# Moving the tail stores and the pooled sums inside the cache loop of a hybrid decoder step

## The chip, the cores and the metric

The kernel runs on one core of one Trainium2 chip. The metric is the device time of one launch in microseconds, as the median of several runs. The core has five engines that work side by side and meet only through semaphores: TensorE (PE, with its weight loads PEld), VectorE (DVE), ScalarE (ACT), GpSimd (POOL) and SyncE (SP). DMAs are issued here from SP, ACT and POOL.

## The reference

The reference is one step of a two-layer decoder trunk on 256 prompt tokens and 8 x 8 sample tokens, all in float32. Each layer computes

```
h   = RMSNorm(x) @ W_in                    # q, k, v | z, xBC, dt | xp
mix = [ StickBreakingAttn(q,k,v) | Mamba2-SSD(z,xBC,dt) | MultiScalePool(xp) ]
x   = x + mix @ W_out
x   = x + W_down( silu(dwconv3(RMSNorm(x) W_gate)) * RMSNorm(x) W_up )
```

The attention of the samples reads 2048 cached tokens a sequence in pages of 128 tokens. `xBC` goes through a causal convolution of width 4, whose last three input rows a sequence are returned (`new_ssm_conv_*`, here the convolution's tails). The pool takes, for four groups of channels, the mean over windows of 2, 4, 8 and 16 tokens minus the token itself, and returns the last 15 input rows a sequence (`new_pool_*`, the pooling's tails). Other results are the keys, the values and the states.

## The kernel before

A layer has four stages with a meeting of all engines between them: the input projection, the mixer (the cache loop), the output projection, and the feed-forward part. The change lies in the mixer alone, which runs once a layer, so twice.

**The cache loop.** Sample attention goes through 128 pages of keys and 128 of values, eight of each a chunk, 16 chunks. The loop is written out by hand as slots: slot s is chunk `qn = s // 8`, position `k = s % 8`. In a slot TensorE transposes one key page (`key_page`, L1122) and multiplies one value page of the chunk two back (`value_page`, L1163), and then does the one step of the rest of the mixer that the table `MIX` (L88) gives for that slot (`step`). ACT, DVE and POOL run through the same slots in the same order, each with its share of the step. The steps' results go alternately into two PSUM banks; TensorE's next step in a bank waits until the one before it was read (`mix_read`).

Steps that matter here: `c` (decays of one quarter of the heads), `y` (SSD output), `s` (the state after the first 128 tokens; ACT copies it into `sT`, L826), `n` (the final prompt state), `pool` (the pool's matmul, L1271), `ctail` (three steps: transpose the convolution's tails, DVE copies them into `ctail`, L1769) and `ptail` (two steps: the pooling's tails of prompt and samples into `ptailP` and `ptail`, L1772). `ctail` and `ptailP` lie in the bytes of `sT`. So ACT may write `sT` at step `("s", 0)`, slot 19, only when all four tail stores have landed (`tail_stored`, L825).

**POOL's queue.** POOL does everything in program order: the loads of value pages (`value_in`, L503; eight buffers; V(q,k) below is page k of chunk q; V(0,k) are loaded ahead of the loop, and V(1,k) is issued at slot 16+k, when TensorE has used V(0,k), and read at slot 24+k), the pooled sums of four groups (`pooled(g)`, L506 to L528: one, two, three and four adds and five instructions behind them, with a drain of the engine after each add), the weighted x of a block (`weighted_x`, L537), the stores of the tails, the gating of y by z (`gate`, L562 to L566, with drains as well) and later the sample states. Before, `pooled` stands at slots 1, 6, 9 and 11, the convolution's stores and the load of `poolw` at slot 13, and the pooling's stores at slot 17.

Of the kernel before, what the change touches and what calls it, by code (L numbers as in the profile page):

```python
# [16 lines left out]
F32 = mybir.dt.float32  # L17
# [29 lines left out]
CVD = SSW + 2 * NG * NS  # L47
# [23 lines left out]
for _t in PARTS:  # L71
# [13 lines left out]
MEETS = 4  # L85


MIX = {0: ("b", 0), 1: ("x", 0, 0), 2: ("x", 0, 1), 3: ("cum", 0), 4: ("dec",), 5: ("ctail", 0),  # L88
# [3 lines left out]
       23: ("b", 1), 24: ("x", 1, 0), 25: ("x", 1, 1), 26: ("cum", 1), 27: ("pool", 0), 28: ("pool", 1), 29: ("pool", 2),  # L92
# [6 lines left out]
for _i in range(2, NB):  # L99
    _s = 67 + 5 * (_i - 2)  # L100
    MIX.update({_s: ("T", _i, 0), _s + 1: ("Y", _i - 1), _s + 2: ("T", _i, 1), _s + 3: ("N", _i - 1, 0),
                _s + 4: ("N", _i - 1, 1)})
# [16 lines left out]
def build(nc, a, o):  # L119

    with ExitStack() as ctx:
        at = [16512]

        def sb_at(name, shape, dt, offset):
            return nc.alloc_sbuf_tensor_at(name, shape, dt, offset=offset)
# [12 lines left out]
        def sem(name):  # L138
            return ctx.enter_context(nc.semaphore(name))


        x = sb("x", [P, KT, TOK])
# [4 lines left out]
        ah_at = at[0]  # L147
# [5 lines left out]
        w_at = at[0]  # L153
# [67 lines left out]
        y = sb_at("y", [P, SST, TOK], F32, hh_at + 4 * TOK * 4)  # L221
# [16 lines left out]
        dec = sb_at("dec", [P, SST, 10], F32, raw_at + 32256)  # L238
        bm = sb_at("bm", [SAMP, 2, NG * NS], F32, ah_at)
        sel = sb_at("sel", [SSH, SST, P], F32, ah_at + 31744)  # L240
        ctail = sb_at("ctail", [27, CVD], F32, w_at + 24576)

        p1 = sb_at("p1", [P, XPL], F32, ah_at + 25600)
        p2 = sb_at("p2", [P, XPL], F32, ah_at + 27520)
# [4 lines left out]
        ptailP = sb_at("ptailP", [PH, POOLW], F32, w_at + 30720)  # L249
        ptail = sb_at("ptail", [P, POOLW], F32, ext_at + 1920)  # L250
# [59 lines left out]
            sem("y_sq"), sem("y_sq_s"), sem("y_ms"), sem("y_root"), sem("y_normed"), sem("y_high"))  # L310
        s_loaded, s_stored = [sem(f"s_loaded{i}") for i in range(4)], [sem(f"s_stored{i}") for i in range(4)]
        s_decayed, s_bm, snew_stored = sem("s_decayed"), sem("s_bm"), sem("snew_stored")
        tail_stored, ftail_T, ftail_out = sem("tail_stored"), sem("ftail_T"), sem("ftail_out")

        passed = sem("passed")
# [3 lines left out]
        def alone(eng):  # L319

            eng.sem_inc(passed, 1)
# [124 lines left out]
        def _(pool):  # L446
# [23 lines left out]
            with pool.Fori(0, DEPTH) as l:  # L470
# [37 lines left out]
                def pooled(g):  # L508

                    win = WINS[g]  # L510
                    src, w, bufs = xp[:, g, :], 1, [p1, p2]
                    while w < win:
                        dst = bufs[0][:]
                        bufs.reverse()
                        pool.tensor_tensor(dst[:, 2 * w - 1:], src[:, 2 * w - 1:], src[:, w - 1:XPL - w], ALU.add)
                        pool.drain()  # L516
                        src, w = dst, 2 * w
                    news = pdiff[:, g, SEQ:TOK].rearrange("p (b t) -> p b t", b=NB)
                    pool.tensor_scalar(pdiff[:, g, 0:SEQ], src[:, PH:PH + SEQ], 1.0 / win, None, ALU.mult)
                    pool.tensor_scalar(news, src[:, SEQ + PH:].rearrange("p (b t) -> p b t", b=NB)[:, :, PH:], 1.0 / win,  # L520
                                       None, ALU.mult)
                    pool.drain()

                    pool.tensor_tensor(pdiff[:, g, 0:16], src[:, PH:PH + 16], con[:, K_CNT + 16 * g:K_CNT + 16 * g + 16],
                                       ALU.mult)
                    pool.drain()
                    pool.tensor_tensor(pdiff[:, g, 0:SEQ], pdiff[:, g, 0:SEQ], xp[:, g, PH:PH + SEQ], ALU.subtract)
                    pool.tensor_tensor(news, news, xps[:, g, :, PH:], ALU.subtract).then_inc(p_diff, 1)  # L528
# [21 lines left out]
                def pool_tails_out():  # L550
                    read(pool, l, "ptail", 0)
                    read(pool, l, "ptail", 1)
                    pool.dma_start(o["new_pool_prompt"][l, 0], ptailP[:]).then_inc(tail_stored, 16)
                    pool.dma_start(o["new_pool_sample"][l].rearrange("b k c -> (b k) c"), ptail[0:NB * PH, :]
                                   ).then_inc(tail_stored, 16)

                def gate(blk):

# [37 lines left out]
                for qn in range(CHUNKS + 3):  # L596
                    for k in range(8):
                        slot = 8 * qn + k
                        if 2 <= qn <= CHUNKS:
                            value_in(qn - 1, k)  # L600
                        if slot in (1, 6, 9, 11):
                            pooled((1, 6, 9, 11).index(slot))
                        for blk in range(3):
                            if slot == SLOT["cum", blk] + 2:
                                weighted_x(blk)
                        if slot == SLOT["ctail", 2] + 1:
                            conv_tails_out()
                        if slot == SLOT["ptail", 1] + 1:
                            pool_tails_out()
                        for blk in range(2):  # L610
                            if slot == SLOT["y", blk, 3] + 1:
                                gate(blk)
                        if slot == SLOT["n", 1] + 1:
                            read(pool, l, "n", 0)
                            read(pool, l, "n", 1)
                            pool.dma_start(o["new_ssm_prompt"][l, 0].rearrange("(j e) p n -> (e p) j n", e=2), snew[:]
                                           ).then_inc(snew_stored, 16)
                        for i in range(NB):
                            if slot == SLOT["N", i, 1] + 1:
                                state_out(i)  # L620
                            if slot == SLOT["T", i, 1] + 1:
                                state_rows(i)
                                state_decay(i)
# [8 lines left out]
                for half in range(2):  # L632
# [5 lines left out]
                pool.dma_start(o["new_ffn_conv_prompt"][l, 0], ftail[0:2, :]).then_inc(tail_stored, 16)  # L638
                pool.dma_start(o["new_ffn_conv_sample"][l].rearrange("b k c -> (b k) c"), ftail[2:18, :]
                               ).then_inc(tail_stored, 16)  # L640
                pool.wait_ge(tail_stored, l * 96 + 96)
                alone(pool)
                meet(pool, "pool", stage(l, M_FFN))
            pool.wait_ge(last_out, 12)
# [7 lines left out]
        def _(act):  # L652
# [51 lines left out]
            with act.Fori(0, DEPTH) as l:  # L704
# [109 lines left out]
                def step(s):  # L814

                    if s not in MIX:
                        return
                    kind, *at = MIX[s]
                    b, bank = USE[MIX[s]][0], ps[MIX_BANKS[USE[MIX[s]][0]]]
                    if kind == "s":  # L820
                        h = at[0]
                        written(act, l, *MIX[s])
                        if h == 0:
                            act.wait_ge(tail_stored, l * 96 + 64)
                            alone(act)  # L825
                        act.activation(s1T[:, h * 512:(h + 1) * 512] if h < 2 else  # L826
                                       sT[:, 1, (h - 2) * 512:(h - 1) * 512], bank[:], ACT.Copy).then_inc(mix_read[b], 1)
                    elif kind == "pool":
                        written(act, l, *MIX[s])
                        act.activation(hh[:, SBT + SST + at[0], :], bank[:, 0:TOK], ACT.Copy,  # L830
                                       scale=par[:, C_PS + at[0]:C_PS + at[0] + 1]).then_inc(p_hi, 1)
                    elif kind == "T":
                        i, h = at
                        written(act, l, *MIX[s])
                        if i >= 2 and h == 0:
                            written(act, l, "Y", i - 2)
                        act.activation(sT[:, i % 2, h * 512:(h + 1) * 512], bank[:], ACT.Copy).then_inc(mix_read[b], 1)

                def exponentials(blk, j):

                    b, bank = USE["c", blk, j][0], ps[MIX_BANKS[USE["c", blk, j][0]]]
                    T, n = tokens(blk)[1], 4 * blk + j
                    act.wait_ge(c_min, l * 12 + n + 1)
                    for i in range(4):
                        mm = act.activation(seg[n % 4][0:T, i, 0:T], seg[n % 4][0:T, i, 0:T], ACT.Exp,
                                            bias=tk[0:T, 2, 4 * j + i:4 * j + i + 1])
                    mm.then_inc(c_exp, 1)
                    if blk:
                        dst = cs[j][:] if blk == 1 else csS[:, 4 * j:4 * j + 4, :]
                        act.activation(dst, bank[:, 0:4 * T].rearrange("p (h t) -> p h t", h=4), ACT.Exp  # L850
                                       ).then_inc(mix_read[b], 1)
# [1165 lines left out]
```

## Time and profile before

| | us |
|---|---|
| median of 3 runs | 3483.42 (3478.25 to 3485.31) |
| profiled execution, its own time | 3491.93 |
| its span in the trace | 3490.4 |
| PE busy | 3264.5 |
| DVE busy | 1921.2 |
| ACT busy | 1338.9 |
| POOL busy | 379.5 |

The profiled execution's own time is its span and 1.5 us around it; it lies 8.5 us above the median of the runs. Times in the trace are counted from the start of the span. The mixer stage of the first layer goes from about 340 to 648 us, that of the second from about 2056 to 2360 us. A row of a timeline has the start, the duration, the engine, the line, the operation with its operands, the count, and in brackets how long the engine was idle before and what it waited for.

### The profile page before, as it was taken

How to read it: one execution, taken by the hardware profiler on the slowest of the kernel's cores; microseconds unless marked ns; L12 is line 12 of the kernel's file. 1: busy time of each engine (PE TensorE's matmuls, PEld its weight loads, DVE VectorE, ACT ScalarE, POOL GpSimd, SP SyncE). 2: the span in 40 equal slices, each digit the busy share in tenths (PEclk: the TensorE clock that was granted, in tenths of full speed). 3: DMA queues.
4: the chain of work that ended last, by engine and by line, in shares of the span. 5: the costliest groups of instructions: out<-in, count | busy, mean ns of one | idle time of the engine just before them, and what ended most of it. 6: DMA issues, size and time to landing. Idle time of an engine off the chain costs nothing.

```text
span 3490.4 us, 66373 instructions
## 1 busy us (share of the span) xinstructions
PE 3264.5 (94%) x23775; PEld 3055.9 (88%) x23775; DVE 1921.2 (55%) x3351; ACT 1338.9 (38%) x1641; POOL 379.5 (11%) x465
## 2 busy tenths in 40 slices
PE   5999899899999999999889988979899999999995
PEld 5999566689999999999879975649899999999994
DVE  5574555346654665466356645454666446645654
ACT  2453555433432333233235535553344333333331
POOL 2000544110000000000020025530200000000000
PEclk8999898899999999999989999999899999999997
DMA  5442698634444444444434437985344444444441
GB/s 154 137 129 91 209 292 284 217 122 133 148 146 155 145 151 150 145 155 132 126 117 133 133 116 220 323 280 169 108 150 145 155 145 151 149 146 155 144 135 44
DMA packets 467566, 553.41 MB, mean 159 GB/s; under 512 B 20044, under 2 KB 413869, under 8 KB 466625
## 3 DMA queue, kind: packets, MB, share of 16 engines
q1 hardware_dynamic: 436354, 461.42, 41.5%
q0 software_dynamic: 26112, 88.93, 8.1%
q8 instruction: 105, 1.72, 0.2%
q10 hardware_dynamic: 4898, 0.55, 0.1%
q14 instruction: 97, 0.79, 0.1%
HBM read 534.46 MB, written 16.38 MB: 158 GB/s over the span
## 4 chain that ended last, share of the span: by engine, by line
PE 86%; issue 4%; DVE 3%; ACT 2%; DMA 1%; POOLq 1%; POOL 1%; DVEq 1%; ACTq 0%
PE ps L937 25%; PE ps L938 25%; PE ps L939 25%; PE ps L1122 2%; PE ps L1163 2%; PE ps L1132 1%; PE ps L1295 1%; PE ps L1283 1%; PE ps L1277 1%; DVE hl L1416 0%; POOLq L516 0%; POOLq L502 0%; DMA xrow<-in_x_sample 0%; PE ps L975 0%; ACT wz L804 0%
## 5 line engine op out<-in xcount | busy, mean ns | idle before, releaser
L1374 DVE TENSOR_TENSOR wl<-raw,wh 128x1024 fp32r<-128x1024 f32 (+1 forms) x752 | 897.5, 1202 | 1100.7 <-ACT wh L659 1093.7
L659 ACT ACTIVATE wh<-raw 128x1024 fp32r<-128x1024 f32 (+1 forms) x752 | 781.4, 1042 | 1680.2 <-PE ps L939 1677.7
L937 PE MATMUL ps<-hh,wh 128*128 128x320 f32 x4224 | 1318.4, 312 | 21.8 <-DVE hl L1416 18.2
L939 PE MATMUL ps<-hh,wl 128*128 128x320 f32 x4224 | 1312.5, 311 | 0.0
L938 PE MATMUL ps<-hl,wh 128*128 128x320 f32 x4096 | 1273.3, 311 | 0.0
L937 PEld LDWEIGHTS ps<-hh,wh 128*128 128x128 f32 x4224 | 799.5, 189 | 30.7 <-DVE hl L1416 23.5
L939 PEld LDWEIGHTS ps<-hh,wl 128*128 128x128 f32 x4224 | 799.8, 189 | 0.0
L938 PEld LDWEIGHTS ps<-hl,wh 128*128 128x128 f32 x4096 | 776.1, 189 | 0.0
L937 PE MATMUL ps<-ah,wh 128*128 128x320 f32 x1408 | 435.3, 309 | 0.1
L938 PE MATMUL ps<-al,wh 128*128 128x320 f32 x1408 | 435.1, 309 | 0.0
L939 PE MATMUL ps<-ah,wl 128*128 128x320 f32 x1408 | 435.1, 309 | 0.0
L937 PEld LDWEIGHTS ps<-ah,wh 128*128 128x128 f32 x1408 | 264.3, 188 | 0.6 <-issue 0.6
L938 PEld LDWEIGHTS ps<-al,wh 128*128 128x128 f32 x1408 | 264.3, 188 | 0.0
L939 PEld LDWEIGHTS ps<-ah,wl 128*128 128x128 f32 x1408 | 264.3, 188 | 0.0
L638 POOL DMA_DIRECT2D out_new_ffn_conv_prompt<-ftail x2 | 1.0, 520 | 1887.9 <-DVE ftail L1931 1887.9
L1122 PE MATMUL ps<-con,kring 128*128 128x128 f32 x1024 | 171.5, 293 | 14.8 <-ACT kT L782 14.8
L503 POOL DMA_DIRECT2D vring<-in_cache_v x256 | 139.2, 544 | 269.4 <-issue 151.2
L1122 PEld LDWEIGHTS ps<-con,kring 128*128 128x128 f32 x1024 | 122.6, 150 | 52.0 <-issue 25.2
L1677 DVE COPY kT<-ps 128x512 f32<-128x512 f32 x128 | 87.9, 687 | 90.1 <-PE ps L1122 87.7
L1163 PE MATMUL ps<-vring,wz 128*32 128x128 f32 x2048 | 113.6, 305 | 20.8 <-ACT wz L804 14.0
L782 ACT ACTIVATE kT<-ps 128x512 f32<-128x512 f32 x128 | 76.0, 594 | 138.9 <-PE ps L1122 138.5
L1163 PEld LDWEIGHTS ps<-vring,wz 128*32 128x32 f32 x2048 | 45.8, 115 | 69.4 <-issue 39.5
(321 smaller groups left out, 3030.5 us busy)
## 6 DMA issues: line engine op xcount, KB each, us to landing
raw<-in_w_gate SPq DMA_DIRECT2D x88, 1024.0 KB, 5.1
raw<-in_w_up SPq DMA_DIRECT2D x88, 1024.0 KB, 5.1
raw<-in_w_in SPq DMA_DIRECT2D x72, 1024.0 KB, 5.2
kring<-in_cache_k SPq DMA_DIRECT2D x256, 256.0 KB, 4.2
vring<-in_cache_v POOLq DMA_DIRECT2D x256, 256.0 KB, 4.4
raw<-in_w_down SPq DMA_DIRECT2D x64, 1024.0 KB, 5.3
raw<-in_w_out SPq DMA_DIRECT2D x32, 1024.0 KB, 5.4
raw<-in_w_down SPq DMA_DIRECT2D x32, 768.0 KB, 4.6
```

Of the source, the lines that this page charges most:

```text
L503: pool.dma_start(vring[:, k, :], a["cache_v"][l, page].rearrange("s h d -> s (h d)")).then_inc(v_loaded[k], 16)
L659: act.activation(wh[:, s % 2, half, :], raw[:, s, half, :], ACT.Copy).then_inc(hi_done, 1)
L782: act.activation(kT[k // 4][:, :, P * (k % 4):P * (k % 4) + P], ps[4][:].rearrange("p (j s) -> p j s", j=SBT), ACT.Copy).then_inc(kT_out[" ...
L937: pe.matmul(out, wh[:, s % 2, kk, w], hi(row), start=first, stop=False)
L938: pe.matmul(out, wh[:, s % 2, kk, w], lo(row), start=False, stop=False)
L939: mm = pe.matmul(out, wl[:, s % 2, kk, w], hi(row), start=False, stop=last)
L1122: mm = pe.transpose(ps[4 + n % 2][:, j * P:(j + 1) * P], kring[:, k, j * P:(j + 1) * P], ident)
L1132: mm = pe.matmul(ps[q % 2][32 * j:32 * j + 32, :], qp[:, q // 4, bb, j, :], kT[bb][:, j, :], start=(bb == 0), stop=(bb == 1))
L1163: mm = pe.matmul(ps[6][32 * j:32 * j + 32, 0:P], wz[:, k // 4, k % 4, j, :], vring[:, k, j * P:(j + 1) * P], start=False, stop=last)
L1277: mm = pe.transpose(bank[:, j * P:(j + 1) * P], s_seq[i % 4][:, 4 * h + j, :], ident)
L1374: dve.tensor_tensor(wl[:, s % 2, half, :], raw[:, s, half, :], wh[:, s % 2, half, :].bitcast(F32), ALU.subtract).then_inc(lo_done, 1)
L1677: dve.tensor_copy(kT[k // 4][:, :, P * (k % 4):P * (k % 4) + P], ps[5][:].rearrange("p (j s) -> p j s", j=SBT)).then_inc(kT_out["dve"], 1)
```

## The change

The convolution's tails and the pooling's tails change places in `MIX`: the pooling's two steps stand at slots 5 and 10 in place of the first two of the convolution's, and the convolution's three at slots 12, 14 and 16. Since POOL's stores follow the last step of each, the pooling's stores are issued at slot 11 (before: 17) and the convolution's at slot 17 (before: 13). The buffer `ctail` moves from the bytes of `sT` to the bytes of `cs[1]` to `cs[3]`, which ACT first writes for block 1. The pooling's stores get a semaphore of their own; ACT waits for it alone before it writes `sT`, and for the convolution's stores before the exponentials of `("c", 1, 1)`, at slot 32. POOL's pooled sums move from slots 1, 6, 9, 11 to 1, 13, 15, 20.

```diff
-MIX = {..., 5: ("ctail", 0), ... 10: ("ctail", 1), 12: ("ctail", 2), 14: ("ptail", 0), 16: ("ptail", 1), ...
+MIX = {..., 5: ("ptail", 0), ... 10: ("ptail", 1), 12: ("ctail", 0), 14: ("ctail", 1), 16: ("ctail", 2), ...
-        ctail = sb_at("ctail", [27, CVD], F32, w_at + 24576)
+        ctail = sb_at("ctail", [27, CVD], F32, ah_at + 8192)
...
# pool_tails_out (POOL): both stores
-  .then_inc(tail_stored, 16)
+  .then_inc(ptail_stored, 16)
...
-                        if slot in (1, 6, 9, 11):
-                            pooled((1, 6, 9, 11).index(slot))
+                        if slot in (1, 13, 15, 20):
+                            pooled((1, 13, 15, 20).index(slot))
...
-                pool.wait_ge(tail_stored, l * 96 + 96)
+                pool.wait_ge(tail_stored, l * 64 + 64)
...
# ACT, step ("s", 0)
-                            act.wait_ge(tail_stored, l * 96 + 64)
+                            act.wait_ge(ptail_stored, l * 32 + 32)
...
# ACT, exponentials(blk, j)
                     act.wait_ge(c_min, l * 12 + n + 1)
+                    if n == 5:
+                        alone(act)
+                        act.wait_ge(tail_stored, l * 64 + 32)
+                        alone(act)
```

## Rows read from the trace of the kernel before

**Rows 1.** Page, part 1 and part 4: busy time, and the chain by engine.
```profile
PE 3264.5 (94%) x23775; PEld 3055.9 (88%) x23775; DVE 1921.2 (55%) x3351; ACT 1338.9 (38%) x1641; POOL 379.5 (11%) x465
...
PE 86%; issue 4%; DVE 3%; ACT 2%; DMA 1%; POOLq 1%; POOL 1%; DVEq 1%; ACTq 0%
```

**Rows 2.** Waits of the whole span: total us, times, longest us.
```profile
ACT sT L826 <- DMA out_new_pool_sample<-ptail: 12.4, 2, 6.6
```

**Rows 3.** Chain of waits, 340 to 660 us: start, us, what.
```profile
385.83 1.14 POOLq L516
396.15 4.28 DMA out_new_pool_sample<-ptail
```

**Rows 4.** Timeline of PE, first layer.
```profile
401.28 2.05 PE L1238 MATMUL ps<-xtok,xw 128*128 128x128 f32 x8 [4.53 <-ACT sT L826]
...
414.93 0.43 PE L1163 MATMUL ps<-vring,wz 128*32 128x128 f32 x8
...
417.99 0.42 PE L1163 MATMUL ps<-vring,wz 128*32 128x128 f32 x8
...
423.78 1.13 PE L1212 MATMUL ps<-con,tk 128*128 128x128 f32 x8 [1.10 <-DVE pool_lo L1779]
...
426.62 0.43 PE L1163 MATMUL ps<-vring,wz 128*32 128x128 f32 x8 [0.83 <-ACT wz L804]
...
431.59 1.16 PE L1247 MATMUL ps<-xtok,xw 128*128 128x128 f32 x8
```

**Rows 5.** Timeline of PE, second layer.
```profile
2117.60 2.05 PE L1238 MATMUL ps<-xtok,xw 128*128 128x128 f32 x8 [5.42 <-ACT sT L826]
...
2134.59 0.43 PE L1163 MATMUL ps<-vring,wz 128*32 128x128 f32 x8
```

**Rows 6.** Timeline of POOL, first layer.
```profile
358.95 0.54 POOL L503 DMA_DIRECT2D vring<-in_cache_v  x1 [0.70 <-issue]
360.19 0.54 POOL L503 DMA_DIRECT2D vring<-in_cache_v  x1 [0.70 <-issue]
...
361.28 0.94 POOL L515 TENSOR_TENSOR p<-xp 128x454 f32<-128x454 f32 x1
364.97 0.86 POOL L519 TENSOR_SCALAR pdiff<-p 128x256 f32<-128x256 f32 x1 [2.75 <-issue]
...
369.54 0.94 POOL L515 TENSOR_TENSOR p<-xp 128x454 f32<-128x454 f32 x1
...
374.81 0.94 POOL L515 TENSOR_TENSOR p<-xp 128x454 f32<-128x454 f32 x1
...
378.83 2.08 POOL L519 TENSOR_SCALAR pdiff<-p 128x256 f32<-128x256 f32 x1 [0.16 <-issue]
...
382.62 0.94 POOL L515 TENSOR_TENSOR p<-xp 128x454 f32<-128x454 f32 x1
...
389.94 0.60 POOL L545 DMA_DIRECT2D out_new_ssm_conv_prompt<-ctail  x1
...
392.87 0.55 POOL L503 DMA_DIRECT2D vring<-in_cache_v  x1 [0.92 <-PE ps L1163]
...
397.61 0.55 POOL L503 DMA_DIRECT2D vring<-in_cache_v  x1 [0.90 <-issue]
...
402.03 1.89 POOL L564 TENSOR_TENSOR z<-y 128x1024 f32<-128x1024 f32 x1 [1.50 <-issue]
...
405.51 0.58 POOL L503 DMA_DIRECT2D vring<-in_cache_v  x1 [0.18 <-issue]
```

**Rows 7.** Tile vring, loads issued from 405 to 408 us.
```profile
DMA to landing us min/median/max: 3.2/3.2/3.3
```

**Rows 8.** DMA issues of the page: KB each, median us to landing.
```profile
vring<-in_cache_v POOLq DMA_DIRECT2D x256, 256.0 KB, 4.4
```

**Rows 9.** Timeline of DVE, first layer.
```profile
373.65 0.67 DVE L1769 COPY ctail<-ps 27x512 f32<-27x512 f32 x1
...
379.00 1.26 DVE L1690 TENSOR_TENSOR_SCAN sq<-rz,sn,lq 128x512 f32<-128x512 f32 x1
```

**Rows 10.** Windows of 2 us: busy us of PE, PEld, DVE, ACT, POOL; PEclk; DMA share; GB/s.
```profile
406.00:408.00 2.00, 2.00 (x21) 1.44 (x20) 0.69 (x1) 1.34 (x3) 0.64 (x2) 0.91 0.82 236
```

More of the change, by code:

```diff
@@ L85 @@
 MEETS = 4
-MIX = {0: ("b", 0), 1: ("x", 0, 0), 2: ("x", 0, 1), 3: ("cum", 0), 4: ("dec",), 5: ("ctail", 0),
[2 rows of a table removed]
+MIX = {0: ("b", 0), 1: ("x", 0, 0), 2: ("x", 0, 1), 3: ("cum", 0), 4: ("dec",), 5: ("ptail", 0),
[2 rows of a table added]
        19: ("s", 0), 20: ("s", 1), 21: ("s", 2), 22: ("s", 3),
@@ L312, in build @@
         s_decayed, s_bm, snew_stored = sem("s_decayed"), sem("s_bm"), sem("snew_stored")
+        ptail_stored = sem("ptail_stored")
         tail_stored, ftail_T, ftail_out = sem("tail_stored"), sem("ftail_T"), sem("ftail_out")
@@ L552, in pool_tails_out @@
                     read(pool, l, "ptail", 1)
-                    pool.dma_start(o["new_pool_prompt"][l, 0], ptailP[:]).then_inc(tail_stored, 16)
+                    pool.dma_start(o["new_pool_prompt"][l, 0], ptailP[:]).then_inc(ptail_stored, 16)
                     pool.dma_start(o["new_pool_sample"][l].rearrange("b k c -> (b k) c"), ptail[0:NB * PH, :]
-                                   ).then_inc(tail_stored, 16)
+                                   ).then_inc(ptail_stored, 16)
                 def gate(blk):
```

4 rows, old and new, of the table MIX are left out of this document.

## The prediction

> **What bounds the kernel now.** I read the page first: the reader sees PE busy for 94% of the span and holding 86% of the chain, POOL with 11% and 1% [rows 1]. So a change on POOL can matter only where PE waits for it. The list of waits has such a place: ACT waits twice, 12.4 us in all, at its copy into `sT` (step `("s", 0)`, slot 19) for a pooling tail's store [rows 2]. The chain shows the same: it runs through the store's DMA, 4.28 us from 396.15 [rows 3]. The timeline of PE has the price: before the `s` matmuls of slot 21 it stood 4.53 us in layer 1 and 5.42 us in layer 2 [rows 4, 5]. The timeline of POOL says why the store was late: `pooled(1)` starts at 369.54, `pooled(2)` at 374.81, `pooled(3)` at 382.62, and the first tail store goes out at 389.94 [rows 6]. POOL is a queue without a gap from 361 to 392 us.
>
> A second price is in the windows: PE's granted clock is 0.91 in the slice from 406, so it came back to the 2.4 GHz level only in that slice, 5 us after PE resumed at 401.28 [rows 4, 10]. An `s` group of 8 matmuls took 2.05 us there and the `n` group of the same shape 1.16 at 431.59 [rows 4]: 43% of 5 us, about 2.1 us, were lost to the lower level. The stall is worth about 4.5 + 2.1 = 6.6 us in layer 1 and 5.4 + 2.1 = 7.5 in layer 2.
>
> **The wait removed.** After the change the pooling's second tail is copied at slot 10, where the convolution's is now: 373.65 + 0.67 = 374.3 [rows 9]. POOL has nothing else to do then. Its idle before a DMA whose wait has just ended is 0.9 us (392.87, [rows 6]); so the stores start at 375.2 and 375.8 and the last lands 4.3 later [rows 3], at 380.1. ACT asks at about 395. This wait is gone, with 15 us to spare. The same holds for the new wait on ACT at slot 32: behind it on ACT stand the exponentials, `cs`, `wz` and key copies, and PE waits for these; but the convolution's stores go out at about 394 and land by 399, and slot 32 is 30 us later. It costs nothing; if the cover went, every microsecond would be PE's. The steps on PE and DVE keep number, shape and order but for 15, 120 and 27 partitions: nothing.
>
> **What is late next.** POOL's queue is now longer where it matters. Every value page V(1,k) of slot 16+k is issued in it, and `pooled(3)` stands between V(1,4) and V(1,5). Drains matter here: `pooled(0)` behind a load issued at 360.19 gets past its first drain only at 364.97, 4.8 us after the issue, with 2.75 us of idle; `gate` behind a load at 397.61 at 402.03, 4.4 us after [rows 6]. `pooled(1)` to `pooled(3)` have no DMA just ahead and no such gap. So I read it that a drain of POOL waits until its own DMAs have landed (landings are 3.2 to 4.4, [rows 7, 8]). Layer 1 then goes, in order:
> - stores 375.2 to 376.3; `pooled(1)`: first add 0.94, drain until 375.8 + 4.3 + 0.5 = 380.6, then the rest of it, 374.81 - 369.54 - 1.08 = 4.2 [rows 6], less some contention: to 384.6.
> - `pooled(2)` takes 7.8 (382.62 - 374.81), of which 1.2 is one instruction of 2.08 where its kind takes 0.86 [rows 6], beside the DVE scan of 379.00 [rows 9]. Its new place has no scan: 6.6, to 391.2. Bounds 6.6 and 7.8.
> - V(1,0), V(1,1): spacing 1.24 (360.19 - 358.95): to 393.7. Convolution's stores and `poolw`: 392.87 - 389.94 = 2.9 to the next load [rows 6], V(1,2) at 396.6 (now 397.61).
> - V(1,2) to V(1,3) with `gate` between: 405.51 - 397.61 = 7.9 [rows 6]: V(1,3) at 404.5, V(1,4) at 405.8.
> - `pooled(3)`: drain until 405.8 + 4.4 = 410.2 (bounds 3.8 and 4.8), then 389.94 - 382.62 - 1.08 = 6.2: V(1,5) is issued at 416.6.
> - It lands 3.3 later, as the two loads did that were issued while PE and the key loads stood still [rows 7]; bounds 3.2 and 4.4 [rows 7, 8]. That is 419.9, between 419 and 422.6.
>
> PE without its stall would ask for V(1,5) (slot 29, now 417.99, [rows 4]) at 417.99 - 6.6 = 411.4, so it stands there for 8.5 us. V(1,3) (now read at 414.93, then 408.3) lands at 407.7 and is in time. So against now PE leaves this point at 419.9 - 418.0 = +1.9 us. The same 5 us at the lower level follow this stall, since it is longer than the old one: +2.1 (0 if the clock held). In exchange DVE and ACT work ahead during it: of the waits of 1.10 and 0.83 us behind slot 29 [rows 4], which come from the scan and the exponentials, I take 1.4 as gone (bounds 0.5 and 1.9). `weighted_x(1)` slides to 427 and is wanted at 431.59 + 2.6: hidden. Layer 1: 1.9 + 2.1 - 1.4 = +2.6 us. Layer 2 has the same pattern 1716.5 us later (2134.59 against 417.99 is 1716.6): +2.5.
>
> Sum: 3491.93 + 5.1 = 3497.0 for the profiled execution, that is, 3488.5 on the median of 3483.42. The larger stall goes away, and the queue of POOL gives it back eight slots later. With all bounds together a layer gives between 1.0 + 0 - 1.9 = -0.9 and 4.6 + 2.1 - 0.5 = +6.2: the forecast's own range is 3481.6 to 3495.8.
>
> The page "SBUF — State Buffer" of the Trainium skill, section "Who interferes with whom", says that a DVE instruction with two SBUF inputs and a GpSimd instruction that reads SBUF exclude each other for their whole length. The trace agrees at one place: 2.08 us for an instruction of 0.86 beside a scan of 1.26 with two SBUF inputs [rows 6, 9]; by it, `pooled(3)` now meets the scan of chunk 2, which gives the slower rival below. The page "DMA: Bandwidth & Descriptors", section "Anatomy of one DMA — SWDGE (gpsimd) path", gives about 2.0 us plus bytes over 436 GB/s, 2.6 us for a value page; the trace has 3.2 at best and 4.4 in the median [rows 7, 8]. By the page each layer would be 0.7 us better; I keep the rows.
>
> **Rivals.**
> *The drains do not wait for landings.* The idle of 2.75 us could be a slow start after eight loads in a row, and 1.50 us the scan's doing. Then POOL is earlier by 3.3 at `pooled(1)`, 1.5 at `gate` and 2.8 at `pooled(3)`: V(1,5) lands at 412.3, 0.9 after PE asks. Gain 5.7 a layer, 11.4 in all: 3472.0. For it: POOL's records are rough. Against it: the gap stands behind the issue of a DMA in both rows, in `gate(1)` and in all three of layer 2, and at no drain without one. Chance 0.13.
> *The shared port and slow landings (the other side: slower).* `pooled(3)` lies on the path and meets the scan of chunk 2 on DVE, `pooled(2)` keeps its 7.8 us, and landings are 4.4 as in the median. Each microsecond from 375 to 420 on POOL is then one on PE, since PE has 8.5 us of idle there to give: V(1,5) lands at 422.6, +4.6 + 2.1 - 1.4 = +5.3 a layer, 10.6 in all: 3494.0. It decides as soon as POOL is 1.0 us later a layer than I have it. For it: the collision that the rows show. Against it: DVE is idle for much of 384 to 396. Chance 0.36.
> *Half way.* V(1,5) is a little late, the clock does not fall: 0 to -3 a layer, about 3480. Chance 0.05; that the pooling's stores stay late enough to hold ACT is below 0.01.
>
> **How the numbers follow.** The forecast has 0.46. 0.2% of the time, 7 us, is about what a measurement of this kernel can tell from no change. The forecast (+5.1) and the half-way case lie within it: 0.51 for the same. The slower rival lies over it: 0.36. The first rival is faster: 0.13. The range from 3475 to 3496 holds the forecast with nearly all its own range, most of the slower rival and none of the faster one.
>
> **What would show it.** Right: ACT's wait at L826 for the store is gone, PE has no idle before the `s` matmuls of slot 21, and a new idle of 7 to 10 us, twice, before a matmul of L1163, for the DMA of a value page; POOL idle 2 to 4 us in `pooled(1)` and `pooled(3)`, right behind the first add; clock at the 1.2 GHz level for some 5 us after the new stall. Wrong: no PE wait of over 2 us on a value page between slots 24 and 31 (then the drains are wrong, and the kernel is faster), or a wait on ACT at L845 for the convolution's stores. A load V(1,5) that lands after 421.5 makes the kernel measurably slower.

## The result, and the profile after

The changed kernel takes 3492.11 us (3485.26 to 3503.38, 12 runs) against 3483.78 (3478.25 to 3489.26, 12 runs) before: ratio 1.0026, 95% interval 1.0016 to 1.0036, 8.3 us slower by the medians and 9.1 by the ratio. The time lies in the range of the prediction (3475 to 3496). It is 3.6 us above the forecast of 3488.5, and over the bound of 0.2% on the slow side.

The waits of the changed kernel (total us, times, longest us) have no row of ACT at the copy into `sT` for a pooling tail; [rows 2] has gone. The waits of PE for value pages have grown. This is their row before and, after the "...", in the changed kernel:

```profile
PE ps L1163 <- DMA vring<-in_cache_v: 6.9, 6, 1.8
...
PE ps L1168 <- DMA vring<-in_cache_v: 27.8, 12, 7.5
```

L1168 is the line of `value_page`, L1163 before. The six waits of before all stand at the end of the mixer (636 to 647 and 2347 to 2357 us), and the changed kernel has waits of that size there too. The timeline of PE in layer 1 and then, after the "...", in layer 2 shows where the new ones stand:

```profile
394.57 1.16 PE L1243 MATMUL ps<-xtok,xw 128*128 128x128 f32 x8
...
408.37 0.43 PE L1168 MATMUL ps<-vring,wz 128*32 128x128 f32 x8 [2.38 <-DMA vring<-in_cache_v]
...
420.82 0.66 PE L1168 MATMUL ps<-vring,wz 128*32 128x128 f32 x8 [7.46 <-DMA vring<-in_cache_v]
...
430.77 0.43 PE L1168 MATMUL ps<-vring,wz 128*32 128x128 f32 x8 [0.58 <-ACT wz L805]
...
2118.45 0.43 PE L1168 MATMUL ps<-vring,wz 128*32 128x128 f32 x8 [2.00 <-DMA vring<-in_cache_v]
...
2131.26 0.66 PE L1168 MATMUL ps<-vring,wz 128*32 128x128 f32 x8 [7.24 <-DMA vring<-in_cache_v]
```

The `s` matmuls now start without a wait and at full speed: 1.16 us for eight, against 2.05 behind a wait of 4.53 [rows 4]. Then PE waits twice a layer for a value page: for V(1,3) (slot 27) 2.4 and 2.0 us, for V(1,5) (slot 29) 7.5 and 7.2 us. The timeline of POOL in layer 1 has the reason:

```profile
374.63 0.60 POOL L554 DMA_DIRECT2D out_new_pool_prompt<-ptailP  x1 [5.75 <-DVE ptail L1777]
...
379.38 2.18 POOL L516 TENSOR_TENSOR p<-p 128x452 f32<-128x452 f32 x1 [2.62 <-issue]
...
384.29 0.94 POOL L516 TENSOR_TENSOR p<-xp 128x454 f32<-128x454 f32 x1
...
390.75 0.60 POOL L504 DMA_DIRECT2D vring<-in_cache_v  x1 [0.61 <-issue]
...
396.47 0.55 POOL L504 DMA_DIRECT2D vring<-in_cache_v  x1 [1.31 <-issue]
397.03 2.38 POOL L563 TENSOR_TENSOR y<-y,z 128x1024 f32<-128x1024 f32 x1
401.68 1.89 POOL L565 TENSOR_TENSOR z<-y 128x1024 f32<-128x1024 f32 x1 [2.27 <-issue]
...
405.14 0.57 POOL L504 DMA_DIRECT2D vring<-in_cache_v  x1 [0.15 <-issue]
406.54 0.55 POOL L504 DMA_DIRECT2D vring<-in_cache_v  x1 [0.83 <-issue]
...
410.86 3.27 POOL L516 TENSOR_TENSOR p<-p 128x452 f32<-128x452 f32 x3 [2.81 <-issue]
...
415.22 0.72 POOL L521 TENSOR_SCALAR pdiff<-p 128x64 f32<-128x64 f32 x1
...
417.91 0.59 POOL L504 DMA_DIRECT2D vring<-in_cache_v  x1 [0.47 <-issue]
```

The reader is to see the idles of 2.62, 2.27 and 2.81 us. Each stands at the first drain behind a DMA that POOL issued itself: the tail stores, V(1,2), V(1,4). Between 406.54 and 417.91 POOL issues no load, since `pooled(3)` stands there; V(1,5) is the load at 417.91. Windows of 2 us of the same kernel (columns as in [rows 10]) have the clock before, during and behind the 7.5 us of idle:

```profile
410.00:412.00 2.00, 1.93 (x13) 0.95 (x12) 0.55 (x1) 1.97 (x4) 1.00 (x2) 0.50 0.10 36
...
414.00:416.00 2.00, 0.00 (x0) 0.00 (x0) 1.81 (x3) 0.00 (x0) 1.69 (x3) 1.00 0.38 85
416.00:418.00 2.00, 0.00 (x0) 0.00 (x0) 0.71 (x1) 0.00 (x0) 1.30 (x4) 0.61 0.13 50
418.00:420.00 2.00, 0.00 (x0) 0.00 (x0) 0.00 (x0) 0.00 (x0) 1.05 (x2) 0.50 0.38 84
...
424.00:426.00 2.00, 2.00 (x15) 0.99 (x13) 0.55 (x1) 1.08 (x3) 0.55 (x2) 0.50 0.58 168
426.00:428.00 2.00, 2.00 (x20) 1.79 (x20) 0.30 (x1) 0.56 (x2) 0.87 (x2) 0.83 0.79 163
```

PE resumes at 420.82 and works at the 1.2 GHz level until some time after 426. The wait of 2.38 us at 408.37 has a dip of its own behind it: the granted clock is 0.50 in the slice from 410 and back at 1.00 in the slice from 414.

**Why the spans don't show it.** The profiled execution took 3491.79 us (span 3490.2), nearly that of before (3491.93 and 3490.4), which lay 8.2 us above its own median. The trace of before has a stretch in the second half of layer 1 in which the granted clock lay at the 1.2 GHz level though PE was fully busy; this is one of the windows there:

```profile
580.00:584.00 4.00, 4.00 (x26) 2.32 (x19) 2.52 (x3) 0.00 (x0) 0.65 (x2) 0.50 0.55 171
```

Such a dip lies elsewhere in each trace: e1's has one at 2274 to 2286 us, e10's one at 2270 to 2282, and the changed kernel's layer 1 has none between 504 and 596. So I compare kernels by where a layer stands, not by its end. POOL issues 128 loads of value pages a layer; here is the time of some of them, in us after the layer's first (layer 1 / layer 2). Counted from 0, load 11 is V(1,3), load 13 is V(1,5), load 36 is issued at slot 44, load 48 at slot 56. Kernels e1 to e10 are the experiments below.

```
kernel   load 11        load 13        load 36          load 48
before   55.01 / 54.55  57.80 / 57.34  110.51 / 110.14  129.46 / 129.11
after    55.12 / 54.23  67.89 / 67.49  114.42 / 113.87  133.55 / 133.00
e1       56.19 / 56.63  59.03 / 59.46  107.19 / 107.37  126.15 / 126.30
e2       53.87 / 52.81  66.14 / 64.89  111.90 / 111.39  131.02 / 130.49
e3       63.25 / 61.79  66.05 / 64.59  113.12 / 111.19  132.05 / 130.12
e4       51.77 / 51.88  64.99 / 64.98  111.18 / 111.47  130.31 / 130.60
e5       47.59 / 47.53  60.65 / 60.24  110.66 / 112.56  132.61 / 132.92
e6       48.63 / 48.91  51.44 / 51.71  109.15 / 109.27  126.50 / 126.51
e7       50.04 / 49.12  52.85 / 51.91  105.90 / 105.76  126.25 / 126.11
e8       47.59 / 48.21  50.40 / 51.02  102.96 / 106.79  123.29 / 124.11
e9       53.63 / 54.08  56.43 / 56.89  102.20 / 103.98  121.16 / 122.92
e10      46.80 / 48.05  49.62 / 50.86  103.36 / 104.09  120.68 / 121.42
```

Before to after at load 36: +3.9 and +3.7 us, 7.6 in all. The medians say 8.3. So nearly the whole loss is made in slots 21 to 44 of the two mixers, and what the rest of the kernel adds does not show beside the spread of the executions.

### The profile page after: what moved, and what is told of

It reads as the page before. It is cut to its first block, busy times and chain, and to the rows that moved or that the text cites. A ratio compares the mean times of both kernels' runs of the same rounds, so it can differ in the third digit from the quotient of the medians.

```text
span 3490.2 us, 66373 instructions
## 1 busy us (share of the span) xinstructions
PE 3259.7 (93%) x23775; PEld 3051.0 (87%) x23775; DVE 1921.1 (55%) x3351; ACT 1338.5 (38%) x1641; POOL 377.8 (11%) x465
## 4 chain that ended last, share of the span: by engine, by line
PE 87%; issue 4%; DVE 3%; ACT 2%; POOLq 1%; DMA 1%; DVEq 1%; ACTq 1%; POOL 0%
PE ps L942 25%; PE ps L943 25%; PE ps L944 25%; PE ps L1127 2%; PE ps L1168 2%; PE ps L1137 1%; PE ps L1300 1%; PE ps L1288 1%; PE ps L1217 1%; PE ps L1282 1%; DVE hl L1421 0%; DMA xrow<-in_x_sample 0%; DMA vring<-in_cache_v 0%; PE ps L980 0%; POOLq L503 0%
## 5 line engine op out<-in xcount | busy, mean ns | idle before, releaser
L1168 PE MATMUL ps<-vring,wz 128*32 128x128 f32 x2048 | 113.5, 305 | 41.4 <-DMA vring<-in_cache_v 27.8
L1168 PEld LDWEIGHTS ps<-vring,wz 128*32 128x32 f32 x2048 | 45.9, 115 | 89.8 <-issue 37.6
```

The source lines that it names most:

```text
L1168: mm = pe.matmul(ps[6][32 * j:32 * j + 32, 0:P], wz[:, k // 4, k % 4, j, :], vring[:, k, j * P:(j + 1) * P], start=False, stop=last)
```

## The experiments

Each time is the median of 11 or 12 executions (e8: 6); ratios are to the kernel before, with their 95% interval.

**e1: the sums at their old slots.** Is it the sums' new place that costs?

```diff
-                        if slot in (1, 13, 15, 20):
-                            pooled((1, 13, 15, 20).index(slot))
+                        if slot in (1, 6, 9, 11):
+                            pooled((1, 6, 9, 11).index(slot))
```

> The changed kernel with the pooled sums back at slots 1, 6, 9, 11; the tails stay swapped and ctail stays in its new place. Theory (the loss is pooled(3) between V(1,4) and V(1,5), with a drain that waits for the loads ahead of it): all sums are over by about 389.5 in layer 1, the pooling's stores start at 390.3 and land at 395, so PE keeps 1 to 2 us of the old stall before slot 21; V(1,3) is issued at about 405 and PE waits for it 1 to 2 us; V(1,5) is issued at about 408 instead of 417.9 and PE does not wait for it. About 5 us faster than before a layer, 10 in all, ratio 0.997. Rival (the swap, the moved ctail or the new waits themselves cost time): a stall of several us stays somewhere else and the time is at or over that of before.

Measured: 3481.16 us (3474.27 to 3484.42), ratio 0.9987 (0.9978 to 0.9996). Faster, but by half of the 10 us expected. PE has no wait left at slot 21, and for V(1,3) it waits longer than the 1 to 2 us expected (4.66 us in layer 2):

```profile
407.68 0.65 PE L1168 MATMUL ps<-vring,wz 128*32 128x128 f32 x8 [3.95 <-DMA vring<-in_cache_v]
```

So the two parts of the change have opposite signs: the tails' new slots and buffers alone gain about 4.5 us (0.9987), and moving the sums on top of them takes 0.9987 to 1.0026.

**e2: the sums moved, the tails as before.** The converse.

```diff
-                        if slot in (1, 6, 9, 11):
-                            pooled((1, 6, 9, 11).index(slot))
+                        if slot in (1, 13, 15, 20):
+                            pooled((1, 13, 15, 20).index(slot))
```

> The kernel before with nothing changed but the pooled sums at slots 1, 13, 15, 20. Theory: both stalls appear. The pooling's stores go out at about 394 and land at 398.8, so PE stands 2 to 3 us before slot 21; V(1,5) is issued at about 417 and lands at 420.5, so PE stands 3 to 5 us at slot 29; 3.5 to 5 us slower than before a layer, ratio 1.002 to 1.003, the same as the whole change. Rival (the spread is what brings the stores forward and is good by itself, the loss comes from the tails' swap): at or under the time of before.

Measured: 3488.83 us (3485.36 to 3500.45), ratio 1.0020 (1.0011 to 1.0029), as expected; at load 36 it is only 2.6 us behind before in both layers together, so not all of this time lies in the stretch under study. PE has both waits (L1238 and L1163 are the lines of before):

```profile
399.51 1.83 PE L1238 MATMUL ps<-xtok,xw 128*128 128x128 f32 x8 [4.28 <-ACT sT L826]
...
419.71 0.42 PE L1163 MATMUL ps<-vring,wz 128*32 128x128 f32 x8 [4.22 <-DMA vring<-in_cache_v]
```

The waits don't add up. With the first one kept, PE arrives later and the second is 4.2 us; with the first one taken away (after) it is 7.5. Both hang on POOL's clock, and PE can't gain ahead of V(1,5).

**e3: the last sum in front of the gate.** Does a drain wait for POOL's own DMAs, or is the idle a matter of these operations?

```diff
-                        if slot in (1, 13, 15, 20):
-                            pooled((1, 13, 15, 20).index(slot))
+                        if slot in (1, 13, 15, 18):
+                            pooled((1, 13, 15, 18).index(slot))
```

> The changed kernel with pooled(3) at slot 18 instead of 20, so just behind V(1,2) and just ahead of gate(0), with no DMA between the two. Theory (a drain of POOL waits until its own DMAs have landed): pooled(3) keeps an idle of 2 to 3 us behind its first add, and gate loses its idle of 2.27 us, because nothing was issued since; V(1,3) is issued at about 413 (now 405.1), V(1,5) at about 415.7 (now 417.9); PE stands about 10 us at slot 27 and leaves slot 29 some 2 us earlier than in the changed kernel: ratio to before about 1.0015. Rival (the idle belongs to the instructions, a slow start or the DVE's port): gate keeps its idle of about 2 us, V(1,5) comes no earlier, ratio 1.0026 or more.

Measured: 3488.90 us (3481.76 to 3494.05), ratio 1.0017 (1.0008 to 1.0026), as expected. `pooled(3)` now stands behind V(1,2), and the gate behind `pooled(3)`, with no DMA between. POOL:

```profile
399.34 3.27 POOL L516 TENSOR_TENSOR p<-p 128x452 f32<-128x452 f32 x3 [3.40 <-issue]
...
405.54 2.34 POOL L563 TENSOR_TENSOR y<-y,z 128x1024 f32<-128x1024 f32 x1
408.02 1.89 POOL L565 TENSOR_TENSOR z<-y 128x1024 f32<-128x1024 f32 x1
```

The gate's idle (2.27 in after) is gone, and `pooled(3)` has the one of its new place. The same instructions idle or don't, by whether a DMA of POOL's is under way. The wait of PE moved to V(1,3), 10.77 us (9.62 in layer 2).

**e4: SP issues the pooling's stores.** The stores leave POOL's queue; their data, slot and semaphore stay.

```diff
-                        if slot == SLOT["ptail", 1] + 1:
-                            pool_tails_out()
...  # SP, at the same slot
+                            sync.dma_start(o["new_pool_prompt"][l, 0], ptailP[:]).then_inc(ptail_stored, 16)
+                            sync.dma_start(o["new_pool_sample"][l].rearrange("b k c -> (b k) c"), ptail[0:NB * PH, :]
+                                           ).then_inc(ptail_stored, 16)
```

> The changed kernel with the two stores of the pooling's tails issued by SP at its slot 11 instead of by POOL. Theory: POOL waits neither for the copy of slot 10 (5.75 us) nor, in pooled(1), for the landing of its stores: the idle of 2.62 us behind the first add of pooled(1) is gone; pooled(2) is over by 381. But pooled(3) still stands behind V(1,4) and keeps its 2.8 us: V(1,5) is issued at about 412.3, lands at 416, and PE stands 5 to 6 us at slot 29. 0 to 2 us faster than before a layer, ratio 0.999 to 1.000. Rival (the idle is a slow start of the first drained add and has nothing to do with POOL's own DMAs): pooled(1) keeps an idle of over 2 us.

Measured: 3485.90 us (3479.84 to 3495.34), ratio 1.0009 (0.9998 to 1.0020): about 6 us better than after, a little less than expected. POOL:

```profile
369.16 0.94 POOL L522 TENSOR_TENSOR p<-xp 128x454 f32<-128x454 f32 x1
370.25 1.20 POOL L522 TENSOR_TENSOR p<-p 128x452 f32<-128x452 f32 x1
...
406.54 3.27 POOL L522 TENSOR_TENSOR p<-p 128x452 f32<-128x452 f32 x3 [2.63 <-issue]
```

`pooled(1)` has no idle at its first drain, where the changed kernel has 2.62, and `pooled(3)`, behind a load, keeps its own. V(1,5) goes out 2.9 and 2.5 us earlier in the two layers (64.99 against 67.89 in the first), and load 36 comes 3.2 and 2.4 us earlier: what POOL gains ahead of V(1,5), PE gets. V(1,5) was issued at 414.20, later than the 412.3 expected, and PE stood 8.9 and 8.7 us for it, not 5 to 6: the gate, whose V(1,2) took 5.1 us to land, idled 2.89 us.

**e5: the gate moved behind the tight stretch.** In the changed kernel and in the next three `gate(0)` stands at slot 35 in place of 18.

```diff
-                            if slot == SLOT["y", blk, 3] + 1:
+                            if slot == (35, SLOT["y", 1, 3] + 1)[blk]:
```

> The changed kernel with gate(0) moved on POOL from slot 18 to slot 35, all else as it is. Theory (POOL's queue between slots 11 and 29 is the path, every microsecond taken out of it comes off the stall at slot 29): the 8 us of gate and its drain leave the queue ahead of V(1,3); V(1,3) is in time (the wait of 2.4 us at slot 27 is gone), pooled(3) keeps its drain, V(1,5) is issued at about 410.5 instead of 417.9 and lands at 414; PE stands 4 to 5 us there instead of 7.5. About 7 us faster than the changed kernel a layer at slot 29, 5 to 6 behind it, ratio to before 0.999. Rival (the stall is the DMA queues' or HBM's, too many loads at once): V(1,5) is issued earlier but lands no earlier, the ratio stays at 1.002.

Measured: 3491.85 us (3485.84 to 3500.86), ratio 1.0018 (1.0007 to 1.0029). A miss. The first half of what was expected happened: load 13 came 7.2 us earlier, and the wait for V(1,5) shrank to 4.2 and 4.9 us. But by load 48 nearly all of that was given back (0.9 and 0.1 us are left). PE:

```profile
414.00 0.65 PE L1168 MATMUL ps<-vring,wz 128*32 128x128 f32 x8 [4.19 <-DMA vring<-in_cache_v]
...
441.11 0.45 PE L1229 MATMUL ps<-seg,xtok 128*64 128x128 f32 x4 [1.89 <-DVE snew L1770]
```

**e6: the same with the sums at 1, 6, 9, 11.**

> The changed kernel with the pooled sums back at 1, 6, 9, 11 and gate(0) at slot 35. Theory: nothing of POOL is left between V(1,2) and V(2,4); no wait on a value page between slots 24 and 31, PE keeps under 1 us before slot 21; the 4 us stall at slot 27 of the kernel with the sums back, and the low clock behind it, are gone. 7 to 8 us faster than before a layer, ratio 0.9955. Rival (gate at slot 35 delays V(3,4) as pooled(3) delayed V(1,5)): a wait of several us on a value page at slot 43 or 44, ratio 0.997 to 0.999.

Measured: 3481.07 us (3474.09 to 3485.94), ratio 0.9987 (0.9977 to 0.9997). A miss again: no wait for a value page is left, and the time is that of e1. At load 13 it was 7.6 us ahead of e1, at load 48 it was not ahead at all. The first part goes at slot 31, where PE waits for DVE:

```profile
415.45 2.04 PE L1217 MATMUL ps<-con,tk 128*128 128x128 f32 x8 [2.71 <-DVE pool_lo L1784]
```

PE had a wait of 1.10 us there in before too [rows 4], and has it in e7 and e10; what is new is the rest. The trace has its reason, in the weighted x of block 1 on POOL (first row) and the scan on DVE (second):

```profile
410.91 1.91 POOL L538 TENSOR_TENSOR xw<-xtok,tk 128x1024 f32<-128x1024 f32 x1
...
411.03 2.88 DVE L1695 TENSOR_TENSOR_SCAN sq<-rz,sq,lq 128x512 f32<-128x512 f32 x1
```

The scan starts just behind the POOL instruction and takes 2.88 us (3.17 in layer 2). In e7 POOL's instruction starts 1.04 us behind the scan, and the same scan takes 1.27:

```profile
411.31 1.27 DVE L1695 TENSOR_TENSOR_SCAN sq<-rz,sq,lq 128x512 f32<-128x512 f32 x1
```

The 1.6 us that the scan loses are those that PE waits more, and behind the wait the granted clock is 0.50 in the slices from 416 and 418: the eight matmuls at 415.45 take 2.04 us, in e10 1.13. Further on, beside the gate, PE waits 0.80 and 1.19 us for DVE's `y`.

**e7: the same with the sums at 1, 6, 13, 15.** These slots put two sums into POOL's idle time, ahead of the stores and behind them.

> The changed kernel with the pooled sums at slots 1, 6, 13, 15 (pooled(1) in POOL's idle ahead of the tail stores, none between the value loads) and gate(0) at slot 35. Theory: the stores go out at 374.6 as in the changed kernel, pooled(2) waits at its first drain for their landing (2 to 3 us), pooled(3) does not; the sums are over by 392, V(1,5) is issued by 402 and no value page is waited for; PE has no stall at slot 21. Ratio 0.9955, the same as with the sums back at 1, 6, 9, 11. Rival (as for the kernel before this one): a wait at slot 43 or 44.

Measured: 3479.91 us (3474.28 to 3491.04), ratio 0.9988 (0.9976 to 0.9999). A miss of the same kind, with the wait of 1.88 us on DVE at 434.23 as in e5.

**e8: e4 and e6 together.** SP issues the pooling's stores, the sums stand at 1, 6, 9, 11, the gate at 35.

> As the kernel with the sums back at 1, 6, 9, 11 and gate(0) at slot 35, and the two stores of the pooling's tails issued by SP. Theory: the stores leave at slot 11 whatever POOL does and land by 382, so ACT's wait at slot 19 is nil; POOL is 1.1 us shorter. Ratio 0.995 to 0.9955, at most 0.0005 better than with the stores on POOL. Rival (SP's wait for the tails' copy delays the key loads behind it): PE waits on a key page between slots 19 and 24.

Measured: 3476.13 us (3472.76 to 3477.73), ratio 0.9970 (0.9958 to 0.9982), better than both kernels. Its trace shows, in layer 1, what e5 and e7 ran into (their traces have the same two DVE instructions at 2.84 or 2.85 and 2.38 us; e6's has the first, at 2.87). POOL first, then DVE:

```profile
421.75 2.37 POOL L569 TENSOR_TENSOR y<-y,z 128x1024 f32<-128x1024 f32 x1
426.18 1.97 POOL L571 TENSOR_TENSOR z<-y 128x1024 f32<-128x1024 f32 x1 [2.06 <-issue]
```

```profile
421.83 2.85 DVE L1819 SCALAR_TENSOR_TENSOR seg<-seg,cbm 128x512 f32<-128x512 f32 x1 [0.27 <-issue]
424.60 0.68 DVE L1826 TENSOR_TENSOR cs<-cs,xc 128x512 f32<-128x512 f32 x1
...
425.72 0.67 DVE L1819 SCALAR_TENSOR_TENSOR seg<-seg,cbm 128x512 f32<-128x512 f32 x1
426.32 2.38 DVE L1826 TENSOR_TENSOR cs<-cs,xc 128x512 f32<-128x512 f32 x1
```

Two DVE instructions that take 0.67 and 0.68 us take 2.85 and 2.38, and both end just behind the POOL instruction beside them (421.75 + 2.37 = 424.1, 426.18 + 1.97 = 428.2). DVE loses 2.2 + 1.7 = 3.9 us, and PE waits for it, 0.84 us for `y` and 1.89 for `snew`. Behind the second wait the granted clock fell (second row, a window):

```profile
430.13 0.45 PE L1233 MATMUL ps<-seg,xtok 128*64 128x128 f32 x4 [1.89 <-DVE snew L1774]
...
432.00:434.00 2.00, 1.69 (x12) 0.78 (x11) 2.00 (x6) 0.63 (x1) 1.46 (x2) 0.50 0.73 217
```

Layer 2 of e8 lost its time elsewhere: its scan took 2.58 us beside the weighted x, as in e6, and PE waited 2.42 us at slot 31.

**e9: e8 with the gate back at slot 18.** Was moving the gate worth anything?

```diff
-                            if slot == (35, SLOT["y", 1, 3] + 1)[blk]:
+                            if slot == SLOT["y", blk, 3] + 1:
```

> The changed kernel with the pooling's stores issued by SP and the pooled sums at slots 1, 6, 9 and 11, and gate(0) left at slot 18. Against e8 it tells what moving gate(0) to slot 35 is worth. Both readings expect the same of POOL: V(1,2) issued at about 394.0 as in e8 (395.2 in e1), gate with its idle of about 2, V(1,3) at about 402.3, V(1,5) at 405.2, and a wait of PE on V(1,3) of about 2.8 us a layer (3.95 in e1), with the 1.2 GHz level after it. Reading A (the gate's move is given back later: beside the n and y steps its operations slow DVE, as e5, e6 and e7 came out no better than their partners): the time is that of e8, ratio 0.997. Reading B (the move is worth the stall of 2.8 and 2.1 for the clock, less what is given back): 3 to 4 us a layer over e8, ratio 0.9985 to 0.999.

Measured: 3474.67 us (3465.75 to 3487.08), ratio 0.9976 (0.9965 to 0.9988). That is e8 within the intervals, and nearer to reading A than to B, whose lower end (0.9985) the interval still holds. The wait for V(1,3) was 0.76 us in layer 1 and 4.26 in layer 2, and only the second one was followed by the lower level of the clock:

```profile
406.97 0.43 PE L1172 MATMUL ps<-vring,wz 128*32 128x128 f32 x8 [0.76 <-DMA vring<-in_cache_v]
...
2107.76 0.65 PE L1172 MATMUL ps<-vring,wz 128*32 128x128 f32 x8 [4.26 <-DMA vring<-in_cache_v]
```

So the gain of e8 over e6, which differ only in who issues the stores (3476.13 against 3481.07, with intervals that overlap a little), does not come from the gate, and the gate's move was worth nothing that shows at slot 35: what PE no longer waits for a page, it waits for DVE.

**e10: the gate at slot 26.** It stands behind the load V(2,2), which PE reads only at slot 34, and ahead of the `n` and `y` steps of block 1.

```diff
-                            if slot == (35, SLOT["y", 1, 3] + 1)[blk]:
+                            if slot == (26, SLOT["y", 1, 3] + 1)[blk]:
```

> e8 with gate(0) at slot 26 in place of 35: behind V(2,2), where the ring of value pages has its eight slots in hand, and before the exponentials' and the n and y steps of block 1. If gate's operations beside DVE's snew and y of slots 34 to 38 gave back time in e8 (waits of PE on DVE snew of 1.9 us), then these waits are gone and V load 36 to 48 takes 19 us rather than 20.3: about 1.5 us a layer better than e8, ratio 0.996. If the given back time is PE's own clock or the chunk's chain on DVE and ACT, which PE reaches 8 us earlier, the place of the gate makes no difference: ratio 0.997. If gate at 406 to 413 slows the scan of chunk 1, the wait of PE for DVE pool_lo at slot 31 (2.4 us in e8) grows by the length of the collision, 1 to 2 us: ratio 0.998.

Measured: 3471.49 us (3464.11 to 3480.15), ratio 0.9965 (0.9955 to 0.9975), the lowest of all, 12 us under the kernel before and some 20 under the changed one. Against e8 load 48 comes 2.6 and 2.7 us earlier, more than the 1.5 expected. The same DVE instruction as above has its own length, the scan takes 1.27 us, and of the waits behind slot 34 in layer 1 one of 0.76 is left, with the granted clock at 1.00 from 400 to 446 us. DVE first, then PE:

```profile
426.01 0.69 DVE L1819 SCALAR_TENSOR_TENSOR seg<-seg,cbm 128x512 f32<-128x512 f32 x1 [0.27 <-issue]
```

```profile
414.20 1.13 PE L1221 MATMUL ps<-con,tk 128*128 128x128 f32 x8 [1.10 <-DVE pool_lo L1788]
...
424.73 0.45 PE L1233 MATMUL ps<-seg,xtok 128*64 128x128 f32 x4 [0.76 <-DVE snew L1774]
```

The intervals of e8, e9 and e10 overlap. That the collision with DVE is gone in e10 is shown; that e10 is faster than e9 is likely, not shown.

## Why the prediction was near, and where it was off

**The wait removed: right.** The stores went out at 374.63 (forecast 375.2), ACT's wait is gone, and PE reaches slot 27 8.4 us ahead of before rather than the 6.6 I reckoned (59.8 us after the stage's first key page against 68.2). The new wait on ACT at slot 32 cost nothing, as said. The price was, if anything, too low.

**Drains wait for POOL's own DMAs: right, and shown.** e3 takes the DMA away from before the gate and the idle goes with it; e4 takes the stores away from before `pooled(1)` and its 2.62 us go. From the issue to the end of the drain it took 4.15 us (after, 375.23 to 379.38) to 5.2 (396.47 to 401.68). The end follows the landing: the stores landed 3.9 us after the issue, V(1,2) 4.8 and V(1,4) 4.1, and the drains ended 0.2, 0.4 and 0.2 us behind. In none of 90 such places in the twelve traces did a drain end ahead of the landing. In most it ended 0.2 to 0.8 us behind; in some 20, all of them at a gate from slot 35 on, up to 1.8 us behind (after, 453.30: landing at 3.4 us, end at 4.9), and that remainder is not explained. Whether the drain waits for the landing itself or for a step of the DMA shortly before it, no run separates. The rival without it (3472.0) is out.

**V(1,3) in time: wrong, without a price of its own.** PE waited 2.4 and 2.0 us for it. I had PE there at 408.3 and the page landed at 407.7 by the old trace; PE was there at 406.0, since it was further ahead and the stage began 0.5 us earlier, and the page was issued 0.6 us later than forecast (405.14 against 404.5). In the changed kernel this costs nothing, because V(1,5) is later anyway, and its issue hangs on POOL alone. In e1, where V(1,5) is on time, this wait is the one that counts (3.95 us with the clock behind it). Whoever stops at the largest new wait misses the next.

**When V(1,5) lands: the term that was mis-sized.** The stage began 0.5 us earlier in the new trace (346.21 against 346.70), so 417.91 answers to 418.4, 1.8 us later than the 416.6 forecast. By the rows shown, V(1,2) was 0.4 late; from it to V(1,3) took 8.67 us and not 7.9, since the gate's drain idled 2.27 and not 1.50; from the end of the drain behind the first add to V(1,5) took 7.05, where the rows gave 6.2 and the forecast's own sum, from 410.2 to 416.6, has 6.4 (it is 0.2 too high as a sum). Of the 0.8 over the rows 0.35 is one instruction of 0.72 us where its like takes 0.37 (415.22), beside this scan on DVE:

```profile
414.46 1.32 DVE L1695 TENSOR_TENSOR_SCAN sq<-rz,sq,lq 128x512 f32<-128x512 f32 x1
```

The rest is the sequencer's time in front of a value load (0.47 us of idle there), which the place that I took the length from ends without. The landing took 2.9 us, not 3.3. The 8.5 us of idle forecast for this place came as two waits, 2.4 and 7.5. Together PE left this place 3.3 us later than before (420.82 - 346.21 against 417.99 - 346.70) where the forecast had +1.9.

**The clock: right in kind.** The clock was at the 1.2 GHz level from the middle of the stall (1.00 in the slice from 414, 0.50 in that from 418) until after 426, 5 to 6 us behind the resumption. At slot 32 PE was 4.6 us behind the kernel before (84.6 against 79.9 after the stage's start), so clock less recovered waits came to +1.3 where I had 2.1 - 1.4 = +0.7. From there on some of it comes back, since waits on ACT become shorter (0.16 and 0.75 us at 459.41 and 461.26 before, 0.48 at 464.87 after): +3.9 at load 36, +4.1 at load 48.

**The sum.** Per layer +3.9 and +3.7 where the prediction had +2.6 and +2.5. The mechanism was the forecast's; the size lies between it and the slower rival (+5.3), whose conditions were partly there: POOL was over the 1.0 us late from which I let it decide, but only 0.35 us of that was the collision with the scan, `pooled(2)` did not keep its 7.8 us (6.5, as forecast), and landings were short. On the chances: with 5.1 us forecast and a bound at 7, an error of 1 us a layer crosses the bound. Giving 0.51 to no change was too sure of one row-by-row sum, when most of what it left out (idle in front of a load, a longer drain) could only add.

**The experiments' misses.** e5 to e7 rested on moving the gate to a place where POOL had time, and looked only at POOL. The gate also took DVE's time where DVE had instructions with two inputs in SBUF, and at slot 35 DVE is what PE waits for next. In e6 the weighted x did the same to the scan. The page "SBUF — State Buffer" of the Trainium skill, section "Who interferes with whom", states that a DVE instruction with two SBUF inputs contends with a GpSimd instruction that reads SBUF, and calls their shared pair of ports an exclusive lock. The trace of e8 agrees, with 2.85 and 2.38 us for instructions of 0.67 and 0.68, and so does that of e6, with 2.88 for a scan of 1.27. I had cited it for POOL's loss and not drawn the other half, DVE's.

**Open.** The collision of the scan with the weighted x in e6 is read from the traces; no run moved `weighted_x(1)` alone. The late dips of the clock under full load were not explained; they move single executions by some us. The two measures used here, medians and the loads up to 48, also differ by more than that: at load 48 e9 is 14.5 us ahead of before and e10 16.5 (both layers), by the medians 8.4 and 11.6. The profiled execution of e9 kept its lead (3467.91, 15 us under the median of before), others of e9 did not (up to 3487.08). Where they lose it was not looked into.

## What to carry to other kernels

When a stall in front of a queue's slowest member is removed, list every load that the queue issues behind it and when the faster consumer asks for each; the gain ends at the first that is late. On POOL, keep compute that drains away from the queue's own DMA issues, or give the DMAs to an engine that doesn't drain: here that was worth about 6 us with not one operation fewer. And price a POOL instruction on DVE too, where DVE is next in line: a start 0.1 us before or 1 us behind a scan decided over 1.6 us.

## What the runs showed of the hardware

- A drain on POOL behind a DMA that POOL issued ended 0.2 to 0.4 us after the landing at the stores, V(1,2) and V(1,4) of the changed kernel's first layer, 4.15 to 5.2 us from the issue; without such a DMA there was no idle (e3, e4).
- A POOL instruction and a DVE instruction with two SBUF inputs stretched each other by up to the whole length of the other: 0.67 to 2.85 us on DVE beside one of 2.37 (e8), 1.27 to 3.17 beside one of 1.91 (e6, layer 2), and 0.37 to 0.72 on POOL (after).
- A stall of 0.76 us left the granted clock at 1.00 in layer 1 of e9, one of 1.89 us (e8, 430.13) and one of 2.4 us (after, 408.37) were followed by the 1.2 GHz level within some 2 us, and before's clock lay at that level from 576 to 584 with PE busy for all 8 us.
